# A second pair of chunks by Strassen's algorithm in four feed forward stages

## The chip, the cores and the metric

The kernel runs on one core of one Trainium2 chip, in one launch. The metric is the device time of that core in microseconds (us), lower is better. The engines are PE (TensorE, with its weight loads as PEld), DVE (VectorE), ACT (ScalarE), POOL (GpSimd) and SP (SyncE, which here only issues transfers).

## The reference, cut to what matters

Two transformer blocks in sequence on 256 tokens of width 1024, all in float32. Five of the kernel's eight stages are feed forward stages of this form (stages 0, 2, 3, 5, 7; the others are mixers):

```
D_FF = ((8 * D_MODEL // 3 + 127) // 128) * 128      # 2816
def swiglu(x, w_in, w_out):
    a, b = jnp.split(x @ w_in, 2, axis=-1)
    return (jax.nn.silu(a) * b) @ w_out
...
f = swiglu(rms_norm(h, g[0]), ffn1_w_in[l], ffn1_w_out[l])
h = h + FFN_RES * rms_norm(f, g[1])
...
ffn = jnp.dot(jax.nn.silu(jnp.dot(h2, w_ffn_gate)) * jnp.dot(h2, w_ffn_up), w_ffn_down)
```

`x` is 256 x 1024, `w_in` 1024 x 5632, `w_out` 2816 x 1024. The second block also needs `silu(c) @ w_ada` (1024 x 6144), a product with one row, which the kernel computes on the side.

## The kernel before, in words

**Splitting.** A float32 product is made of three matmuls on rounded parts: weights and activations are each written as hi + lo, and hi·hi, hi·lo and lo·hi are summed in PSUM. Every piece of weights, called a sub here (two blocks of 128 rows by 512 columns, 128x1024 on the chip), is loaded, rounded by ACT (line 549, `whi`), and its rest is taken by DVE (line 560, `wlo`). PE then runs 12 matmuls with it (lines 757, 758, 760): 2 row blocks x 2 halves of the tokens x 3. Seven split buffers (`NSPL`) let ACT and DVE run ahead of PE; `act_begin(j)` and `dve_begin(j)` split up to sub j + 4 (`ahead`), and the split of sub j waits until PE is done with sub j - 7. Raw weights come through a ring of three 1 MB buffers that SP fills (line 522): a refill waits for the `wlo` of the unit three places earlier. A unit is 1 MB, two subs.

**A feed forward stage.** The 2816 hidden columns are 11 chunks of 256; with both matrices a chunk is 512 columns, four subs, 48 matmuls, in one PSUM bank for each half of the tokens (tok 0, tok 1). Six banks (`acc`) go round in a ring, so a chunk's banks come back two chunks later. When a chunk ends, ACT takes silu of one half (line 1161), DVE multiplies by the other (`dve_gate`, line 1167) and signals `gated`, which frees the bank. Pairs of chunks are transposed on PE (line 1225) and split again by ACT and DVE (`gh`, `gl`: lines 1240, 1249) for the down product.

**Strassen.** In stages 2, 3, 5 and 7 the chunks 8 and 9 are computed together: a 256 x 1024 by 1024 x 1024 product, seen as 2 x 2 blocks, takes seven block products (p1 to p7) of 12 matmuls each instead of eight. Their subs are sums of weight blocks: POOL issues plain transfers (line 587) and accumulating ones (line 585) into the buffers `rows` (x1) and `work` (x2), and DVE makes one sum (`dve_t2`, line 576). The sums of activation blocks (`sxh`, `sxl`) are made by DVE and ACT at set places in chunks 3 to 5 (`SX_AT`, `SX_HI`, `SX_LO`; lines 618 to 640). ACT copies partial results (`act_part`, line 878), DVE subtracts them in PSUM (`dve_combine`, line 887), and both finish with `act_silu_pair` and `dve_gate_pair` (lines 1184, 1191). p1 stands before chunk 10, the other six between subs of the down product (`BESIDE`).

**On the side.** `w_ada` comes in 96 tiles (12 groups of 8), one beside a ring unit where `ADA_UNITS` allows it by the unit's number in its stage. DVE adds tile k right after a unit's last `wlo` (`ada_add`: k = 0 at line 651, the others at 654). After a group's eighth tile SP writes the sum out in four transfers (line 684), and k = 0 of the next group waits until they have landed (`s_sent`), because it overwrites the same buffer; later five small DVE instructions fold the group (`ada_sum`, lines 661 to 670).

**Order.** Every engine's program is written out in order by hand, and each engine runs its own strictly in that order; semaphores tie them together.

## Time and profile before

| | us |
|---|---|
| time, median of 3 runs | 1409.75 (1408.96 to 1410.26) |
| the profiled execution's own time | 1410.26 |
| its span in the profile | 1408.5 |
| PE busy | 1394.6 (99%) |
| DVE busy | 1003.0 (71%) |
| ACT busy | 760.9 (54%) |
| granted TensorE clock, mean | 0.999 of full |

Busy time of PE counts overlapping matmuls, so 99% says only that PE hardly ever stands idle. DVE and ACT shares are averages over stages; whether one of them is late somewhere is seen in the order of time. Idle time of an engine other than PE costs nothing unless PE waits for what is behind it.

### The profile page before, as it was taken

What the parts mean: (1) busy time and instruction counts of PE and PEld (TensorE: products, weight loads), DVE (VectorE), ACT (ScalarE), POOL (GpSimd) and SP (SyncE); (2) the same over time, 40 slices, a digit from 0 to 9 for tenths busy, and PEclk for the clock granted to TensorE, in tenths of its full rate; (3) what the DMA queues carried; (4) which work ended last, traced back from release to release, by engine and by line L of the source; (5) the groups of instructions that cost most, each with busy time, mean ns of one, the idle gap of its engine ahead of it and who ended that gap; (6) DMA issues with size and microseconds to landing.
All of it is one profiled execution on the core that took longest, in us unless ns stands there. A gap on an engine that the chain in (4) does not pass through costs nothing.

```text
span 1408.5 us, 19150 instructions
## 1 busy us (share of the span) xinstructions
PE 1394.6 (99%) x7293; PEld 1141.1 (81%) x7293; DVE 1003.0 (71%) x1350; ACT 760.9 (54%) x1080; POOL 195.4 (14%) x272
## 2 busy tenths in 40 slices
PE   9999999999999999999999999999999999999998
PEld 7888888688888888888878888888877788788886
DVE  6667666887867678676786877766568666776664
ACT  5444455665555455454755645556556634655452
POOL 1600010010001010010172101101652110000100
PEclk9999999999999999999999999999999999999999
DMA  9777756148879688787544788784745355586672
GB/s 311 245 237 234 258 183 209 61 140 267 278 193 273 212 264 258 238 231 234 182 142 150 226 272 254 196 264 143 255 149 195 120 179 179 196 252 210 170 217 92
DMA packets 228346, 294.54 MB, mean 209 GB/s; under 512 B 35156, under 2 KB 142480, under 8 KB 228256
## 3 DMA queue, kind: packets, MB, share of 16 engines
q1 hardware_dynamic: 218992, 272.04, 59.7%
q0 software_dynamic: 8832, 20.97, 6.9%
q8 instruction: 58, 0.95, 0.3%
q10 hardware_dynamic: 432, 0.32, 0.1%
q14 instruction: 32, 0.26, 0.1%
HBM read 289.09 MB, written 4.20 MB: 208 GB/s over the span
## 4 chain that ended last, share of the span: by engine, by line
PE 93%; DVE 3%; issue 2%; ACT 1%; DMA 1%; SPq 0%; POOL 0%; POOLq 0%; ACTq 0%; DVEq 0%
PE ps L757 27%; PE ps L760 27%; PE ps L758 27%; PE ps L864 2%; PE ps L863 2%; PE ps L862 2%; PE pst L1225 1%; PE pst L1041 1%; DVE wlo L560 1%; PE pst L1558 1%; DMA raw<-in_ffn_w_in_dram 0%; ACT whi L549 0%; PE ps L1505 0%; PE pst L1872 0%; DMA ada_out<-adaacc 0%
## 5 line engine op out<-in xcount | busy, mean ns | idle before, releaser
L560 DVE TENSOR_TENSOR wlo<-raw,whi 128x1024 fp32r<-128x1024 f32 (+2 forms) x450 | 540.3, 1224 | 178.4 <-ACT whi L549 174.6
L549 ACT ACTIVATE whi<-raw 128x1024 fp32r<-128x1024 f32 (+2 forms) x450 | 450.3, 1039 | 130.8 <-PE ps L760 115.6
L757 PE MATMUL ps<-whi,xh 128*128 128x512 f32 (+2 forms) x1310 | 513.7, 392 | 1.8 <-DVE wlo L560 0.9
L758 PE MATMUL ps<-wlo,xh 128*128 128x512 f32 (+2 forms) x1310 | 503.8, 385 | 0.0
L760 PE MATMUL ps<-whi,xl 128*128 128x512 f32 (+2 forms) x1310 | 495.3, 385 | 0.0
L757 PEld LDWEIGHTS ps<-whi,xh 128*128 128x128 f32 x1310 | 245.9, 188 | 56.9 <-issue 3.7
L760 PEld LDWEIGHTS ps<-whi,xl 128*128 128x128 f32 x1310 | 245.9, 188 | 49.8
L758 PEld LDWEIGHTS ps<-wlo,xh 128*128 128x128 f32 x1310 | 246.2, 188 | 46.0
L757 PE MATMUL ps<-whi,gh 128*128 128x512 f32 x440 | 172.7, 392 | 0.0
L758 PE MATMUL ps<-wlo,gh 128*128 128x512 f32 x440 | 171.3, 389 | 0.0
L760 PE MATMUL ps<-whi,gl 128*128 128x512 f32 x440 | 153.4, 389 | 0.0
L1161 ACT ACTIVATE hid<-ps,st 128x256 f32<-128x256 f32 x76 | 36.0, 473 | 164.6 <-PE ps L760 164.6
L760 PEld LDWEIGHTS ps<-whi,gl 128*128 128x128 f32 x440 | 82.6, 188 | 17.3
L757 PEld LDWEIGHTS ps<-whi,gh 128*128 128x128 f32 x440 | 82.6, 188 | 17.3 <-DVE hid L1191 0.2
L758 PEld LDWEIGHTS ps<-wlo,gh 128*128 128x128 f32 x440 | 82.7, 188 | 16.7
L981 POOL TENSOR_SCALAR st<-st 128x1 f32<-128x1 f32 x26 | 11.6, 446 | 562.4 <-ACT work L967 562.4
L1167 DVE SCALAR_TENSOR_TENSOR hid<-ps,st,hid 128x256 f32<-128x256 f32 x76 | 35.9, 482 | 70.8 <-ACT hid L1161 70.7
L654 DVE SCALAR_TENSOR_TENSOR adaacc<-adat,scol,adaacc 128x512 f32<-128x512 f32 x84 | 62.7, 747 | 6.3 <-DMA adat<-in_w_ada_dram 6.3
L1240 ACT ACTIVATE gh<-pst 128x1024 fp32r<-128x1024 f32 x25 | 25.7, 1028 | 44.6 <-PE pst L1225 44.6
L549 ACT ACTIVATE whi<-rows 128x1024 fp32r<-128x1024 f32 x32 | 32.9, 1054 | 17.9 <-PE ps L760 13.3
L560 DVE TENSOR_TENSOR wlo<-rows,whi 128x1024 fp32r<-128x1024 f32 x32 | 38.1, 1220 | 4.8 <-ACT whi L549 4.7
L1249 DVE TENSOR_TENSOR gl<-pst,gh 128x1024 fp32r<-128x1024 f32 x25 | 30.5, 1220 | 10.0 <-ACT gh L1240 10.0
(315 smaller groups left out, 1253.4 us busy)
## 6 DMA issues: line engine op xcount, KB each, us to landing
raw<-in_ffn_w_in_dram SPq DMA_DIRECT2D x150, 512.0 KB, 5.1
raw<-in_ffn_w_out_dram SPq DMA_DIRECT2D x40, 1024.0 KB, 6.4
raw<-in_w_in_dram SPq DMA_DIRECT2D x26, 1024.0 KB, 5.0
adat<-in_w_ada_dram SPq DMA_DIRECT2D x96, 256.0 KB, 5.8
raw<-in_hyb_w_in_dram SPq DMA_DIRECT2D x10, 1024.0 KB, 5.3
raw<-in_gla_w_in_dram SPq DMA_DIRECT2D x10, 1024.0 KB, 5.2
raw<-in_w_ffn_down_dram SPq DMA_DIRECT2D x10, 1024.0 KB, 7.4
rows<-in_ffn_w_in_dram POOLq DMA_DIRECT2D x18, 512.0 KB, 5.9
```

The source lines that it names most:

```text
L549: e.activation(split_of(whi, j), raw_of(j), ACT.Copy).then_inc(*whi_made.up(j))
L560: e.tensor_tensor(split_of(wlo, j), raw_of(j), split_of(whi, j).bitcast(F32), ALU.subtract).then_inc(*wlo_made.up(j))
L654: e.scalar_tensor_tensor(adaacc[:, :], adat[n % 2][:, :], sc, adaacc[:, :], ALU.mult, ALU.add).then_inc(*ada_added.up(c, k))
L757: e.matmul(ps[:, 0:n], a, whi_of(j, k), start=first and k == 0, stop=False)
L758: last = e.matmul(ps[:, 0:n], a, wlo_of(j, k), start=False, stop=False)
L760: last = e.matmul(ps[:, 0:n], b, whi_of(j, k), start=False, stop=final and k == subs[j][2] - 1)
L862: e.matmul(ps[:, :], a, whi_of(j, k), start=first and not i and not k, stop=False, skip_group_check=True)
L863: e.matmul(ps[:, :], a, wlo_of(j, k), start=False, stop=False, skip_group_check=True)
L864: last = e.matmul(ps[:, :], b, whi_of(j, k), start=False, stop=i == 1 and k == 1, skip_group_check=True)
L1161: e.activation(hb[:, tok * 512 + 256:tok * 512 + 512], acc.of(st, JC[st, c], tok)[:, 0:256], ACT.Silu, scale=rstd(("h", st, tok)) if st < ...
L1167: e.scalar_tensor_tensor(hb[:, tok * 512:tok * 512 + 256], acc.of(st, JC[st, c], tok)[:, 256:512], rstd(("h", st, tok)) if st < 7 else 1.0 ...
L1249: e.tensor_tensor(halves_of(gl[:, x]), turned_halves, halves_of(gh[:, x]).bitcast(F32), ALU.subtract).then_inc(*glo_made.up(st, c))
```

## The change

`STRASSEN` stays (2, 3, 5, 7), and in all four (`TWO`) the chunks 4 and 5 are now a second Strassen pair. Its seven products stand among the chunks of the first product; the order of a stage becomes 0, 1, p1, 2, p2, 3, p5, 6 (with p6 inside), p3, 7, p7, 10 (with p4 inside), and the pair 8, 9 has p1 moved to the start of the down product. The pair 4, 5 takes fixed PSUM banks 4, 0, 3, 2, and every single chunk from 2 on the fixed banks 1 and 5. The buffers x1 and x2 change roles for the second pair, whose p5 starts with its own plain load of a block (`pool_first`) that POOL waits for. The activation sums move forward to chunks 1 and 2. Transposes of hidden pairs move to (2, 2), (6, 3), (10, 1) and behind chunk 10. In the form of `ADA_UNITS` nothing changes, but a stage now has 29 ring units where it had 31, and so takes 21 tiles where it took 22.

```diff
         STRASSEN = (2, 3, 5, 7)
-        PAIR = 8
+        TWO = (2, 3, 5, 7)
...
+        OTHER = {"x1": "x2", "x2": "x1", "ring": "ring"}
         BESIDE = {2: ("p5",), 4: ("p6",), 6: ("p3", "p2"), 10: ("p7",), 12: ("p4",)}
+        INSIDE = {(6, 2): (4, "p6"), (10, 2): (4, "p4")}
...
         def sequence(st):
 
+            if st in TWO:
+                return (0, 1, (4, "p1"), 2, (4, "p2"), 3, (4, "p5"), 6, (4, "p3"), 7, (4, "p7"), 10)
             if st in STRASSEN:
-                return (*range(8), "p1", 10)
+                return (*range(8), (8, "p1"), 10)
             return tuple(range(11))
...
+        def pool_first(e, st, pair):
+
+            u, v = product_unit[st, pair, "p5"], product_unit[st, pair, "p1"]
+            buf, landed = buffer_of(u)
+            for half in range(2):
+                e.dma_start(buf[:, half * 1024:(half + 1) * 1024].rearrange("p (k n) -> p k n", k=2),
+                            plan[v][0][0][0][:, 2 * half:2 * half + 2, :]).then_inc(*landed[half].up(u, "first"))
+            for half in range(2):
+                e.wait_ge(*landed[half].at(u, "first"))
...
         def pool_strassen(e, st):
...
+                pool_product(e, st, 4, "p1", False)
+                split(4, "p1")
+                pool_product(e, st, 4, "p5", True)
+                e.wait_ge(*xlo_made.at(st, "sums", 1))
+                pool_product(e, st, 4, "p3", False)
+                split(4, "p6")
+                pool_product(e, st, 4, "p4", True)
+                split(4, "p3")
+                pool_product(e, st, 4, "p7", True)
+                split(4, "p7")
+                pool_first(e, st, 8)
+                pool_product(e, st, 8, "p5", True)
+                split(4, "p4")
+                pool_product(e, st, 8, "p3", False)
+            split(8, "p6")
+            pool_product(e, st, 8, "p4", True)
+            split(8, "p3")
+            pool_product(e, st, 8, "p7", True)
...
+            ta, tb_, tc, td = (4, 0, 3, 2) if pair == 4 else (0, 3, 1, 5)
...
+        def turns_at(st, c, i):
+
+            if st in TWO:
+                return {(2, 2): 0, (6, 3): 2, (10, 1): 6}.get((c, i))
+            return before(st, c) if c % 2 == 0 and i == 2 else None
...
-                mixed = c == 10 and st in STRASSEN
-                pe_chunk(e, st, JC[st, c], readers[c], at, (acc.n + 1, acc.n + 5) if mixed else (None, None))
+                mixed = st in TWO or c == 10 and st in STRASSEN
+                pe_chunk(e, st, JC[st, c], readers[c], at, (acc.n + 1, acc.n + 5) if mixed else (None, None), CSUB[st, c])
+            if st in TWO:
+                pe_hid_two(e, st, 4)
...
-        SX_AT = [(3, 0), (3, 1), (3, 2), (3, 3), (4, 0)]
-        SX_HI, SX_LO = [(5, 0), (5, 2)], [(5, 1), (5, 3)]
+        SX_AT = {False: [(3, 0), (3, 1), (3, 2), (3, 3), (4, 0)], True: [(1, 0), (1, 1), (1, 2), (1, 3), (2, 0)]}
+        SX_HI = {False: [(5, 0), (5, 2)], True: [(2, 1), (2, 2)]}
+        SX_LO = {False: [(5, 1), (5, 3)], True: [(2, 2), (2, 3)]}
+
+        COMBINE = {(2, 2): "p1", (6, 3): "p6", (10, 1): "p7"}
...
+                    if twice and (c, i) in COMBINE and c > 2:
+                        dve_combine(e, st, 4, COMBINE[c, i])
+                    if twice and (c, i) == (10, 2):
+                        dve_glo(e, st, 6)
+                        dve_gate_pair(e, st, 4, 0)
+                    if twice and (c, i) == (10, 3):
+                        dve_gate_pair(e, st, 4, 1)
```

PE in stage 3, before, from the end of chunk 2 to the first matmuls of chunk 3 (numbers are buffers; lines 757 to 760 are the three matmuls, L1225 the transposes). Left out are rows of the same kind:

```order
L757 MATMUL ps2<-whi2,xh 128x512 [waits wlo_made]
...
L760 MATMUL ps3<-whi2,xl 128x512
L757 MATMUL ps4<-whi3,xh 128x512 [waits wlo_made,gated]
...
L757 MATMUL ps5<-whi3,xh 128x512 [waits gated]
...
L757 MATMUL ps4<-whi4,xh 128x512 [waits wlo_made]
```

A chunk goes to the next pair of banks in the ring. PE in stage 3, after, at the same place, with the block product p2 of the pair 4, 5 (L925) between chunk 2 and chunk 3:

```order
L822 MATMUL ps5<-whi3,xl 128x512
L925 MATMUL ps0<-whi4,xh 128x512 [waits wlo_made,part_made]
...
L925 MATMUL ps0<-whi5,xh 128x512 [waits wlo_made]
...
L819 MATMUL ps1<-whi6,xh 128x512 [waits wlo_made,gated]
...
L819 MATMUL ps5<-whi6,xh 128x512 [waits gated]
```

Chunk 3 now writes ps1 and ps5, the banks that chunk 2 wrote, and waits there for chunk 2's gates, with 12 matmuls of p2 in between.

DVE in stage 3, before, from the gates of chunk 1 to the gates of chunk 2 (L1167 gate, L560 wlo, L654 tile of w_ada, L661 to L670 fold, L1249 gl):

```order
L654 SCALAR_TENSOR_TENSOR adaacc<-adat,scol,adaacc 128x512 [waits ada_added,s_ada1]
...
L651 TENSOR_SCALAR adaacc<-adat,scol 128x512 [waits s_sent,silu_c,s_ada0]
L560 TENSOR_TENSOR wlo<-raw,whi 128x1024 [waits whi_made] x2
L654 SCALAR_TENSOR_TENSOR adaacc<-adat,scol,adaacc 128x512 [waits ada_added,s_ada1]
L1167 SCALAR_TENSOR_TENSOR hid<-ps,st,hid 128x256 [waits silu_made] x2
L560 TENSOR_TENSOR wlo<-raw,whi 128x1024 [waits whi_made] x2
L654 SCALAR_TENSOR_TENSOR adaacc<-adat,scol,adaacc 128x512 [waits ada_added,s_ada0]
L661 TENSOR_TENSOR fold<-fold 128x256 [waits s_fold]
...
L560 TENSOR_TENSOR wlo<-raw,whi 128x1024 [waits whi_made] x2
L654 SCALAR_TENSOR_TENSOR adaacc<-adat,scol,adaacc 128x512 [waits ada_added,s_ada1]
L1249 TENSOR_TENSOR gl<-pst,gh 128x2x8x64 [waits ghi_made]
L1167 SCALAR_TENSOR_TENSOR hid<-ps,st,hid 128x256 [waits silu_made] x2
```

DVE in stage 3, after, from the last tile of a group (L716) over the gates of chunk 1 (L1233) to those of chunk 2; L591 is wlo, L713 the first tile of the next group, L689 and L692 steps of the activation sums, L702 their lo part, L1324 gl:

```order
L716 SCALAR_TENSOR_TENSOR adaacc<-adat,scol,adaacc 128x512 [waits ada_added,s_ada1]
L689 TENSOR_TENSOR work<-work 128x512 [waits summed]
L1233 SCALAR_TENSOR_TENSOR hid<-ps,st,hid 128x256 [waits silu_made] x2
L591 TENSOR_TENSOR wlo<-raw,whi 128x1024 [waits whi_made] x2
L713 TENSOR_SCALAR adaacc<-adat,scol 128x512 [waits s_sent,silu_c,s_ada0]
L591 TENSOR_TENSOR wlo<-raw,whi 128x1024 [waits whi_made]
L692 TENSOR_TENSOR work<-work 128x512 [waits summed]
...
L702 TENSOR_TENSOR sxl<-work,sxh 128x1024 [waits xhi_made]
L591 TENSOR_TENSOR wlo<-raw,whi 128x1024 [waits whi_made]
L716 SCALAR_TENSOR_TENSOR adaacc<-adat,scol,adaacc 128x512 [waits ada_added,s_ada0]
...
L702 TENSOR_TENSOR sxl<-work,sxh 128x1024 [waits xhi_made]
L1324 TENSOR_TENSOR gl<-pst,gh 128x2x8x64 [waits ghi_made]
L1233 SCALAR_TENSOR_TENSOR hid<-ps,st,hid 128x256 [waits silu_made] x2
```

The group's first tile (L651, now L713), which waits for `s_sent`, stood before the gates of chunk 1 and now stands behind them, and the steps of the activation sums have come in between the two pairs of gates.

## Rows read from the trace of the kernel before

**Rows 1.** the page, parts 1 and 4, busy times and the chain that ended last

```profile
PE 1394.6 (99%) x7293; PEld 1141.1 (81%) x7293; DVE 1003.0 (71%) x1350; ACT 760.9 (54%) x1080; POOL 195.4 (14%) x272
...
PE 93%; DVE 3%; issue 2%; ACT 1%; DMA 1%; SPq 0%; POOL 0%; POOLq 0%; ACTq 0%; DVEq 0%
```

**Rows 2.** waits, longest first: engine line waited for, us, times, longest (engines PE, DVE)

```profile
PE ps L818 <- ACT whi L549: 1.4, 1, 1.4
...
PE pst L1225 <- DVE hid L1191: 0.5, 1, 0.5
...
DVE adaacc L651 <- DMA ada_out<-adaacc: 20.9, 6, 5.0
```

**Rows 3.** windows of stages 2, 3, 5, 7: busy us (count) by engine, clock, DMA share, GB/s

```profile
305.00:481.00 176.00, 176.00 (x849) 144.56 (x848) 134.79 (x158) 94.57 (x119) 15.58 (x16) 1.00 0.82 251
487.00:665.00 178.00, 178.00 (x858) 146.34 (x857) 136.19 (x159) 96.30 (x121) 15.39 (x16) 1.00 0.80 241
782.00:958.00 176.00, 175.50 (x847) 144.13 (x846) 132.43 (x153) 94.29 (x119) 13.63 (x16) 1.00 0.82 248
1214.00:1384.00 170.00, 169.68 (x816) 138.94 (x816) 120.32 (x142) 95.49 (x125) 10.83 (x11) 1.00 0.71 217
```

**Rows 4.** timeline of ACT: silu of tok 1 in stages 3 (chunks 1, 2, 3) and 7

```profile
515.45 0.47 ACT L1161 ACTIVATE hid<-ps,st 128x256 f32<-128x256 f32 x1 [2.60 <-PE ps L760]
...
527.21 0.47 ACT L1161 ACTIVATE hid<-ps,st 128x256 f32<-128x256 f32 x1 [0.88 <-PE ps L760]
...
538.09 0.47 ACT L1161 ACTIVATE hid<-ps,st 128x256 f32<-128x256 f32 x1 [0.88 <-PE ps L760]
...
1241.55 0.38 ACT L1161 ACTIVATE hid<-ps 128x256 f32<-128x256 f32 x1 [2.36 <-PE ps L760]
```

**Rows 5.** timeline of DVE, stage 3: prices of its instructions and one wait

```profile
505.78 0.75 DVE L654 SCALAR_TENSOR_TENSOR adaacc<-adat,scol,adaacc 128x512 f32<-128x512 f32 x1
...
507.79 0.49 DVE L1167 SCALAR_TENSOR_TENSOR hid<-ps,st,hid 128x256 f32<-128x256 f32 x1 [1.27 <-ACT hid L1161]
...
514.93 0.49 DVE L651 TENSOR_SCALAR adaacc<-adat,scol 128x512 f32<-128x512 f32 x1 [3.83 <-DMA ada_out<-adaacc]
...
515.33 2.35 DVE L560 TENSOR_TENSOR wlo<-raw,whi 128x1024 fp32r<-128x1024 f32 x2
...
517.60 0.74 DVE L654 SCALAR_TENSOR_TENSOR adaacc<-adat,scol,adaacc 128x512 f32<-128x512 f32 x1
...
518.26 0.87 DVE L1167 SCALAR_TENSOR_TENSOR hid<-ps,st,hid 128x256 f32<-128x256 f32 x2
...
521.98 0.42 DVE L661 TENSOR_TENSOR fold<-fold 128x256 f32<-128x256 f32 x1
...
523.51 2.35 DVE L560 TENSOR_TENSOR wlo<-raw,whi 128x1024 fp32r<-128x1024 f32 x2
...
526.44 1.22 DVE L1249 TENSOR_TENSOR gl<-pst,gh 128x1024 fp32r<-128x1024 f32 x1
...
532.74 0.69 DVE L621 TENSOR_TENSOR work<-work 128x512 f32<-128x512 f32 x1
```

**Rows 6.** timeline of DVE, stage 7: the last gate of chunk 0

```profile
1235.17 0.43 DVE L1167 SCALAR_TENSOR_TENSOR hid<-ps,hid 128x256 f32<-128x256 f32 x1 [1.46 <-ACT hid L1161]
```

**Rows 7.** lines 585 (accumulating, whole run) and 587 (plain, 315 to 330 us): time to landing

```profile
DMA to landing us min/median/max: 5.8/9.2/12.4
...
DMA to landing us min/median/max: 4.2/4.4/4.7
```

**Rows 8.** timeline of DVE, stage 5: the same waits for a transfer out

```profile
853.63 0.75 DVE L654 SCALAR_TENSOR_TENSOR adaacc<-adat,scol,adaacc 128x512 f32<-128x512 f32 x1
...
864.95 0.49 DVE L651 TENSOR_SCALAR adaacc<-adat,scol 128x512 f32<-128x512 f32 x1 [5.02 <-DMA ada_out<-adaacc]
...
939.53 0.74 DVE L654 SCALAR_TENSOR_TENSOR adaacc<-adat,scol,adaacc 128x512 f32<-128x512 f32 x1
...
947.28 0.49 DVE L651 TENSOR_SCALAR adaacc<-adat,scol 128x512 f32<-128x512 f32 x1 [3.59 <-DMA ada_out<-adaacc]
```

275 lines of the change are left out of this document (161 added, 114 removed).

## The prediction

> **What bounds the kernel now.** I read the page first: PE is busy for 1394.6 us of the span and carries 93% of the chain that ended last, DVE 3% [rows 1]. Then the waits: PE's longest is one of 1.4 us at the start of the kernel, and inside the four stages it is 0.5 us, once [rows 2]. So time is what PE issues, plus nothing. Then the windows of the four stages that change [rows 3]: PE is busy throughout, DVE for 134.8 of 176 us in stage 2, 136.2 of 178 in stage 3, 132.4 of 176 in stage 5, 120.3 of 170 in stage 7 (77, 77, 75 and 71%), ACT for about 95. The reader is to see that DVE has a quarter left on average; whether it has that quarter where the change puts work is a question for the order of time. There the opening of a stage is the tight place: from the first tile after its wait in stage 3 to the first step of the activation sums behind chunk 3, DVE's rows follow each other without a gap (514.93 to 532.74) [rows 5], though some work of that stretch was held up by a transfer (3.83 us of waiting).
>
> **What the change takes away.** A pair of chunks costs 2 x 4 subs x 12 = 96 matmuls, seven products of 12 cost 84. That is 12 matmuls a stage, 48 in four stages. Two chunks without anything between them end 538.09 - 527.21 = 10.88 us apart [rows 4], so a matmul takes 10.88 / 48 = 0.2267 us, and 48 of them 10.9 us. The transposes are as many as before; a chunk with one group of them takes 527.21 - 515.45 = 11.76 us [rows 4], 0.88 more. The gain is therefore 10.9 us if PE stays gapless.
>
> **What it adds off PE, per stage.** Seven products need 14 splits where two chunks needed 8. On DVE a wlo takes (517.60 - 515.33) / 2 = 1.135 us from start to start, a tile of w_ada 0.66 (517.60 to 518.26), two gates about 0.8, the fold 1.53 (521.98 to 523.51), a gl or any other 128x1024 sum 1.13, a step of the activation sums 0.60 after overlap [rows 5]. Six more wlo are 6.8 us, the weight sum of 128x2048 is two such sums, 2.2, two combines 1.2, and two pair gates in place of four small ones give back 0.3: 9.9 us. DVE goes to some 144 of 173 us in stage 2. ACT gets 6 splits and three copies more, about 8 on 95 us. Both fit on average, so neither becomes the bound of a stage. POOL's transfers: 6 MB for the new pair in place of 4, and 1 MB for the second pair's own first block. Each lands 4.2 to 4.7 us after a plain issue in the opening and 5.8 to 12.4 after an accumulating one [rows 7]. Walking the order, p7 of the pair 4, 5 has the least room (its split is due about 11 us after its transfer can start, against 5.8 to 12.4), but ACT and DVE then are four subs ahead of PE, which hides even the 12.4. I take 0 for all transfers; bounds 0 and 1.4 us (12.4 less 11) a stage, if the lead has been used up.
>
> **The new wait.** Before, a chunk's banks came back two chunks later. Now chunk 3 needs the banks of chunk 2, chunk 6 those of 3, and so on, with one product between. From the last matmul of a bank's half to its next first one there are 18 others, 4.3 us from start to start. Silu and gate (0.47 and 0.49) follow the half's last matmul; with its own time I reckon 1.4 us when ACT and DVE are free. So DVE may be 2.9 us late at a gate, not more; behind the gate's wait stands all of PE. The Trainium skill speaks against such a layout (Perfetto Trace Analysis, Optimizing Tensor Performance: independent groups of matmuls should go round through different PSUM banks, so that the evacuation of one overlaps the next). By it alone each of the 16 places would show a bubble; by the rows a bubble of 0 is left wherever DVE is on time, and the sum below goes by the rows.
>
> **Where DVE is late: chunk 2 to chunk 3.** PE needs the first gate of chunk 2 at (silu of tok 1 of chunk 1, less 0.2 us) + p1 2.72 + chunk 2 with its transposes 11.76 + p2 2.72: 17.0 us after that silu. Between the last gate of chunk 0 (508.28 in stage 3, 7.17 before the silu at 515.45 [rows 4, 5]) and the gate wanted, DVE now has ten wlo 11.35, five steps of the activation sums 1.13 + 4 x 0.60, their two lo parts 2.26, gl 1.13, three gates 1.2: 19.5 us. To this come tiles and fold, which differ. It also waits 0.5 to 0.9 us for the first hi part of p1, whose transfer is just landing.
> - Stage 2: four tiles 2.6, fold 1.5: 23.6 + 0.8 - 7.17 = 17.3 us. Stop of PE 0.3 us.
> - Stage 5: four tiles, no fold: 15.6. No stop.
> - Stage 7: four tiles and a fold, and the start (1235.60) is only 5.95 us before the silu at 1241.55 [rows 4, 6], because that stage issues its opening in another order: 17.95. Stop 1.0 us.
> - Stage 3: here a group of w_ada ends in between. The next group's first tile waits until the four transfers out have landed: 514.93 - 506.53 = 8.4 us after the end of the eighth tile in stage 3 [rows 5], 864.95 - 854.38 = 10.6 and 947.28 - 940.28 = 7.0 us in stage 5 [rows 8]. Before, it stood in front of chunk 1's gates and cost nothing. Now the eighth tile ends at about 516.8, DVE comes to the first tile at 520.4 and waits until 525.2, with 12.2 us of work from there to the gate: 537.4, where PE wants it at 515.45 + 17.0 = 532.45. Stop 5.0 us; with 7.0 and 10.6 it is 3.5 and 7.2.
>
> **Other places, from the same order.** In stage 5 a group starts between the two pair gates of the pair 4, 5. With A the end of p7 on PE, the eighth tile ends at A + 7.8; 7.0 to 8.4 later plus 0.4 and 0.75 the second pair gate is done at A + 16.0 to 17.4. PE wants it for the transposes at A + 14.5 (p4, chunk 10 and one group of transposes). Stop 1.5 to 2.9, I take 2.2, and 5.1 with the 10.6. The other group start of stage 5 holds DVE up ahead of chunk 3's gates: 0 to 1.4, I take 0.3. Stage 3 has a fold ahead of its pair gate: 0 to 0.5, I take 0.2. Against this, stage 5's stop of 0.5 us before its last transposes [rows 2] goes, since no group starts there any more. Chunks 6, 7 and 10 otherwise have 1.5 us and more of room.
>
> **The sum.** Against the profiled execution, 1410.26 us (span 1408.5 and 1.8 around it): - 10.9 + 0.3 + 5.0 + 1.0 + 2.2 + 0.3 + 0.2 - 0.5 = - 2.4, so 1407.9. This execution lies 0.5 us above the median of the runs, so I forecast 1407.5 for a median. A change within 0.2% (2.8 us, 1406.9 to 1412.6) is what a measurement of this kernel can't tell from none. With the low ends (3.5 + 1.5, the rest 0, less 0.5) it is -6.4, or 1403.4; with the high ends (1.4 in stage 2 and in stage 7 for transfers besides 0.3 and 1.0, 7.2, 5.1, 1.4, 0.5) it is +6.9, or 1416.7.
>
> **Rivals.**
> 1. *The stops don't appear.* The walk packs DVE without any choice; if ACT or the transfer out is quicker by 2 us, or if the group's wait ends with the 7.0 of a calm stretch and the stage's lead takes up the rest, stops come to under 5 us: - 6 to - 10.9, 1399 to 1403.8, centre 1402. For it: PE waited for a gate only 0.5 us in the four stages of before, though DVE was loaded there too. Against it: the bank is a hard wait, and stage 3's order leaves DVE no gap.
> 2. *The stops last long enough to slow PE's clock*, which ends on the other side. Every window of the trace has a granted clock of 1.00 [rows 3], the upper level of 2.4 GHz, and PE never stood idle there for more than 0.5 us; the stop in stage 3 would be ten times that. At the lower level, 1.2 GHz, matmuls issued back to back take twice as long: a sub 5.4 instead of 2.7 us. Bounds are one sub (+ 2.7) and a chunk (+ 10.9); I take two subs and a half, + 6.8, which gives 1414.3. [...] The Trainium skill's page TensorE: Matmul & The Clock Gate (HAM oscillation) describes this mechanism, idle gaps between bursts that bring the clock down; no row of before shows it.
> 3. *The edge is DMA*, with 3 MB more in each stage: DMA share 0.82 at 251 GB/s in stage 2 [rows 3], so 7% more load gives 0.88. If landings move from 4.4 to 8 us in the opening, p1's hi part is 3.6 us late in each stage, and so is all of DVE behind it: + 3.6 in stages 2, 3 and 7, + 2.3 in stage 5, 13 in all: 1420. Against it: the same p1 transfer was issued at the same place before.
> 4. *Nothing is changed in matmuls*: excluded, the order has 48 fewer.
>
> **Chances.** Forecast (stops of 5 to 11 us) 57%, rival 1 22%, rival 2 14%, rival 3 7%. Of the forecast's 57, 22 fall below 1406.9 and 34 within 0.2%. Faster: 22 + 22 = 44%. Same: 34 and a few of rival 2, 37%. Slower: 19%. The range 1401.5 to 1414 leaves out part of rival 1 and the upper half of rivals 2 and 3. The forecast's own range is 1403.5 to 1411.
>
> **What would show it.** Waits of PE (its matmul into the chunk's banks, line 819 of the new kernel) for DVE's gate at line 1233: one of about 5 us in stage 3 between p2 and chunk 3, none there in stage 5, about 1 in stage 7; a wait of the transposes for the pair gate (line 1257) of about 2 us in stage 5; DVE's first tile (line 713) waiting 4 to 5 us for the transfer out just before the long one. I am wrong if these waits add up to under 4 or over 12 us, if PE's matmuls are not 10.9 us less, if the clock leaves 1.00, or if PE waits for wlo instead of for gates.

## The result, and the profile after

| | before | changed |
|---|---|---|
| time, median us | 1409.75 | 1442.77 (5 runs, 1439.66 to 1446.58) |
| ratio to before | | 1.0236, 95% interval 1.0225 to 1.0247 |
| profiled execution, us (its span) | 1410.26 (1408.5) | 1439.66 (1437.9) |
| matmuls of PE | 7293 | 7245 |

The change costs 33 us where a gain of 2.4 us was forecast, and the time lies outside the range. The profiled execution is the fastest of the five, 29.4 us of span above the one before; what follows explains those 29.4. The other four are slower at the same or a lower mean clock (0.985 to 0.988, the profiled one 0.988); where their further time goes is not shown. The page of the changed kernel (busy time and count, then shares of the chain that ended last; compare [rows 1]):

```profile
PE 1397.9 (97%) x7245; PEld 1140.5 (79%) x7245; DVE 1040.9 (72%) x1378; ACT 786.7 (55%) x1108; POOL 238.3 (17%) x312
...
PE 77%; DVE 9%; DMA 6%; issue 3%; SPq 2%; ACT 2%; POOL 0%; POOLq 0%; ACTq 0%; DVEq 0%
```

PE has 48 matmuls less and is busy for 3.3 us more. DVE's part of the chain has grown from 3 to 9%, that of transfers from 1 to 6%. The waits (us in total, times, longest), which stand against [rows 2]; the last line is of the kernel before:

```profile
DVE adaacc L713 <- DMA ada_out<-adaacc: 41.1, 7, 9.3
...
PE ps L819 <- DVE hid L1233: 12.9, 6, 3.4
...
DVE adaacc L716 <- DMA adat<-in_w_ada_dram: 11.3, 9, 4.7
PE pst L1300 <- DVE hid L1257: 11.2, 2, 7.7
...
PE ps L925 <- ACT ps L943: 3.1, 1, 3.1
...
DVE adaacc L654 <- DMA adat<-in_w_ada_dram: 6.3, 2, 3.2
```

PE now waits 24.1 us for DVE's gates and 3.1 us for a copy by ACT, 27.2 us where it waited 0.5. DVE's wait at a group's first tile (L713) for the transfer out has doubled, and at ordinary tiles (L716) DVE waits 11.3 us in nine places where it waited 6.3 in two (L654). PE's stops one by one, from the timeline of PE (start of the matmul, then in brackets how long PE stood before it):

```profile
349.10 0.50 PE L819 MATMUL ps<-whi,xh 128*128 128x512 f32 x1 [0.82 <-DVE hid L1233]
...
411.74 0.71 PE L1300 MATMUL pst<-cst,hid 64*128 64x64 f32 x16 [3.46 <-DVE hid L1257]
...
535.67 0.52 PE L925 MATMUL ps<-whi,xh 128*128 128x512 f32 x1 [3.07 <-ACT ps L943]
...
543.70 0.80 PE L819 MATMUL ps<-whi,xh 128*128 128x512 f32 x1 [3.43 <-DVE hid L1233]
...
593.57 0.50 PE L819 MATMUL ps<-whi,xh 128*128 128x512 f32 x1 [2.38 <-DVE hid L1233]
...
844.60 0.50 PE L819 MATMUL ps<-whi,xh 128*128 128x512 f32 x1 [1.03 <-DVE hid L1233]
...
860.87 0.50 PE L819 MATMUL ps<-whi,xh 128*128 128x512 f32 x1 [2.22 <-DVE hid L1233]
...
914.19 1.12 PE L1300 MATMUL pst<-cst,hid 64*128 64x64 f32 x16 [7.75 <-DVE hid L1257]
...
1287.74 0.80 PE L819 MATMUL ps<-whi,xh 128*128 128x512 f32 x1 [3.07 <-DVE hid L1233]
```

Two in stage 2, three in stage 3, three in stage 5, one in stage 7. At L819 PE wants a shared bank of a single chunk, at L1300 it wants the gated pair for its transposes. What DVE did ahead of the two in the middle of stage 3 (timeline of DVE; compare [rows 5]):

```profile
518.48 0.75 DVE L716 SCALAR_TENSOR_TENSOR adaacc<-adat,scol,adaacc 128x512 f32<-128x512 f32 x1
...
519.75 0.87 DVE L1233 SCALAR_TENSOR_TENSOR hid<-ps,st,hid 128x256 f32<-128x256 f32 x2
...
530.88 0.49 DVE L713 TENSOR_SCALAR adaacc<-adat,scol 128x512 f32<-128x512 f32 x1 [7.99 <-DMA ada_out<-adaacc]
...
540.90 1.22 DVE L702 TENSOR_TENSOR sxl<-work,sxh 128x1024 fp32r<-128x1024 f32 x1
542.04 1.22 DVE L1324 TENSOR_TENSOR gl<-pst,gh 128x1024 fp32r<-128x1024 f32 x1
543.17 0.87 DVE L1233 SCALAR_TENSOR_TENSOR hid<-ps,st,hid 128x256 f32<-128x256 f32 x2
```

The eighth tile ends at 519.23, DVE reaches the next group's first tile 3.66 us later and stands there for 8.0 us: the transfer out took 11.65 us where the prediction had 8.4. From 530.88 to the gate at 543.17 it is 12.3 us of work with one gap of 0.3, as forecast (12.2). ACT, which the prediction had not followed there, was held up by the same wait, because its split of the activation sums comes ahead of its copy of p1 into the bank in which p2 adds up:

```profile
533.13 1.06 ACT L697 ACTIVATE sxh<-work 128x1024 fp32r<-128x1024 f32 x1 [10.71 <-DVE work L692]
...
535.04 0.58 ACT L943 ACTIVATE ps<-ps 128x512 f32<-128x512 f32 x1
```

Then the clock. Windows of 2 us over the same place (columns as in [rows 3]):

```profile
536.00:538.00 2.00, 2.00 (x6) 1.60 (x5) 1.96 (x3) 2.00 (x3) 0.00 (x0) 0.51 0.96 301
...
544.00:546.00 2.00, 2.00 (x5) 1.52 (x5) 2.00 (x3) 0.00 (x0) 0.00 (x0) 0.50 0.93 295
...
550.00:552.00 2.00, 2.00 (x10) 1.64 (x9) 2.00 (x2) 0.35 (x1) 0.00 (x0) 1.00 0.89 324
```

After 3.1 us of standing PE works at 0.51, half of full speed, which is the level of 1.2 GHz; a window of 2 us touches 6 matmuls where it touches 10 at 1.00. With such windows over the whole span, the time lost to the lower level (1 less the granted clock, times PE's busy time, where the clock is under 0.99) is 13.1 us, in six intervals. Each begins during one of these stops or at most 1.5 us behind it. These sums are good to about 0.2 us. The Trainium skill (TensorE: Matmul & The Clock Gate, HAM oscillation) describes idle gaps between bursts that bring the clock down; here the trace agrees.

Each stage, from its first transpose of x to that of the next (stage 7: to its last matmul), adds up:

| stage | before | changed | difference | matmuls | stops | lower clock | sum |
|---|---|---|---|---|---|---|---|
| 2 | 183.6 | 187.0 | + 3.5 | - 2.7 | + 4.3 | + 1.7 | + 3.3 |
| 3 | 183.5 | 196.6 | + 13.0 | - 2.7 | + 8.9 | + 6.3 | + 12.5 |
| 5 | 182.9 | 193.1 | + 10.2 | - 2.7 | + 10.5 | + 2.1 | + 9.9 |
| 7 | 188.4 | 191.8 | + 3.5 | - 2.7 | + 3.1 | + 3.0 | + 3.3 |

(Stage 5's stops are 11.0 us less the 0.5 that it had before.) So the 10.9 us of matmuls were saved, and 27 us of stops and 13 of lower clock came on top. The experiments are about what makes DVE late.

### The profile page after: what moved, and what is told of

It is laid out like the page before. It is cut to its first block, busy times and chain, and to the rows that moved or that the text cites. A ratio compares the mean times of both kernels' runs of the same rounds, so it can differ in the third digit from the quotient of the medians.

```text
span 1437.9 us, 19194 instructions
## 1 busy us (share of the span) xinstructions
PE 1397.9 (97%) x7245; PEld 1140.5 (79%) x7245; DVE 1040.9 (72%) x1378; ACT 786.7 (55%) x1108; POOL 238.3 (17%) x312
## 4 chain that ended last, share of the span: by engine, by line
PE 77%; DVE 9%; DMA 6%; issue 3%; SPq 2%; ACT 2%; POOL 0%; POOLq 0%; ACTq 0%; DVEq 0%
PE ps L819 21%; PE ps L822 21%; PE ps L820 21%; DVE wlo L591 4%; DMA adat<-in_w_ada_dram 3%; PE ps L925 3%; PE ps L926 3%; PE ps L927 3%; DMA ada_out<-adaacc 2%; SPq L746 2%; PE pst L1107 1%; ACT whi L580 1%; PE pst L1300 1%; DVE adaacc L716 1%; PE pst L1666 1%
## 5 line engine op out<-in xcount | busy, mean ns | idle before, releaser
L591 DVE TENSOR_TENSOR wlo<-raw,whi 128x1024 fp32r<-128x1024 f32 (+3 forms) x434 | 521.4, 1225 | 167.4 <-ACT whi L580 163.6
L580 ACT ACTIVATE whi<-raw 128x1024 fp32r<-128x1024 f32 (+3 forms) x434 | 436.6, 1040 | 167.2 <-PE ps L822 132.0
L819 PE MATMUL ps<-whi,xh 128*128 128x512 f32 (+4 forms) x1182 | 467.3, 395 | 14.6 <-DVE hid L1233 12.9
L820 PE MATMUL ps<-wlo,xh 128*128 128x512 f32 (+4 forms) x1182 | 456.8, 386 | 0.0
L822 PE MATMUL ps<-whi,xl 128*128 128x512 f32 (+4 forms) x1182 | 448.2, 387 | 0.0
L819 PEld LDWEIGHTS ps<-whi,xh 128*128 128x128 f32 x1182 | 223.7, 189 | 67.4 <-DVE hid L1233 15.5
L822 PEld LDWEIGHTS ps<-whi,xl 128*128 128x128 f32 x1182 | 223.6, 189 | 45.5
L820 PEld LDWEIGHTS ps<-wlo,xh 128*128 128x128 f32 x1182 | 224.1, 190 | 41.7
L819 PE MATMUL ps<-whi,gh 128*128 128x512 f32 x440 | 172.6, 392 | 0.0
L819 PEld LDWEIGHTS ps<-whi,gh 128*128 128x128 f32 x440 | 82.6, 188 | 17.1
L716 DVE SCALAR_TENSOR_TENSOR adaacc<-adat,scol,adaacc 128x512 f32<-128x512 f32 x84 | 62.8, 747 | 11.3 <-DMA adat<-in_w_ada_dram 11.3
L591 DVE TENSOR_TENSOR wlo<-rows,whi 128x1024 fp32r<-128x1024 f32 x48 | 57.3, 1221 | 8.2 <-ACT whi L580 8.2
L1233 DVE SCALAR_TENSOR_TENSOR hid<-ps,st,hid 128x256 f32<-128x256 f32 x64 | 29.6, 480 | 41.3 <-ACT hid L1227 41.3
L580 ACT ACTIVATE whi<-work 128x1024 fp32r<-128x1024 f32 x40 | 41.5, 1060 | 32.3 <-PE ps L822 12.6
L591 DVE TENSOR_TENSOR wlo<-work,whi 128x1024 fp32r<-128x1024 f32 x40 | 47.7, 1220 | 11.3 <-ACT whi L580 11.2
```

The lines of the kernel that those rows point to most:

```text
L580: e.activation(split_of(whi, j), raw_of(j), ACT.Copy).then_inc(*whi_made.up(j))
L591: e.tensor_tensor(split_of(wlo, j), raw_of(j), split_of(whi, j).bitcast(F32), ALU.subtract).then_inc(*wlo_made.up(j))
L716: e.scalar_tensor_tensor(adaacc[:, :], adat[n % 2][:, :], sc, adaacc[:, :], ALU.mult, ALU.add).then_inc(*ada_added.up(c, k))
L819: e.matmul(ps[:, 0:n], a, whi_of(j, k), start=first and k == 0, stop=False)
L820: last = e.matmul(ps[:, 0:n], a, wlo_of(j, k), start=False, stop=False)
L822: last = e.matmul(ps[:, 0:n], b, whi_of(j, k), start=False, stop=final and k == subs[j][2] - 1)
```

## The experiments

The expectations weigh theories by letter. A: DVE's wait at a group's first tile makes the gates late. A2: any wait of DVE for a transfer of w_ada ahead of a gate does. B: DVE has too much work of its own. C and D: transfers are late as a whole, wherever the work that needs them stands. E: SP's long issue of the transfer out holds up what it issues next.

Ratios are to the kernel before, on the same chip; "stops" are PE's of 0.6 us and more in the four stages, "clock" is the time lost to the lower level, both of the profiled execution. Runs of different groups ran on different chips, so a difference between groups is surer in the ratios than in us.

| run | median us | ratio, 95% interval | stops | clock |
|---|---|---|---|---|
| changed kernel | 1442.77 | 1.0236 (1.0225 to 1.0247) | 27.2 | 13.1 |
| two_acc | 1437.49 | 1.0201 (1.0187 to 1.0215) | 21.1 | 7.1 |
| two_acc_gates_first | 1432.20 | 1.0164 (1.0150 to 1.0178) | 16.5 | 6.8 |
| two_acc_aligned | 1424.63 | 1.0105 (1.0091 to 1.0119) | 19.7 | 7.2 |
| two_acc_gates_aligned | 1422.73 | 1.0091 (1.0075 to 1.0106) | 15.7 | 7.8 |
| tiles_moved | 1432.32 | 1.0161 (1.0148 to 1.0175) | 23.8 | 4.7 |
| three_edits | 1411.03 | 1.0004 (0.9994 to 1.0014) | 8.4 | 3.3 |
| folds_moved | 1407.22 | 0.9980 (0.9970 to 0.9990) | 5.4 | 0 |
| plain_out | 1421.98 | 1.0091 (1.0077 to 1.0105) | 17.9 | 8.6 |
| plain_edits | 1408.33 | 0.9991 (0.9982 to 1.0000) | 6.1 | 1.5 |
| no_dma_wait | 1406.37 | 0.9976 (0.9966 to 0.9986) | 5.1 | 1.4 |
| no_wait_no_load | 1406.45 | 0.9975 (0.9966 to 0.9984) | 5.7 | 1.7 |
| seven_only | 1412.68 | 1.0019 (1.0010 to 1.0028) | 3.9 | 1.6 |
| five_seven | 1415.68 | 1.0048 (1.0035 to 1.0061) | 8.0 | 1.6 |
| before_two_acc | 1418.27 | 1.0063 (1.0050 to 1.0077) | 0 | 0 |
| before_moved_480 | 1418.89 | 1.0065 (1.0052 to 1.0079) | 0 | 0 |
| before_edits | 1409.08 | 0.9997 (0.9989 to 1.0006) | 0 | 0 |
| before_plain | 1412.02 | 1.0017 (1.0008 to 1.0026) | 2.6 | 0 |

**Two accumulators for w_ada**, so that a group's first tile no longer waits for the transfer out of the group just ended. They were built twice. `st_` is cut to 384 columns in both; with `mhalf` as below the tiles behind end up 1,056 bytes on, with `mhalf` as a part of `st_` (`st_[:, 376:384]`, the aligned version) 1,024 bytes:

```diff
-        adaacc = sb("adaacc", 512)
+        adaacc = [sb(f"adaacc{i}", 512) for i in range(2)]
...
-        mhalf = sb("mhalf", P)[:, 0:8]
+        mhalf = sb("mhalf", 8)
...
-                if c:
-                    e.wait_ge(*s_sent.at(c - 1))
+                if c > 1:
+                    e.wait_ge(*s_sent.at(c - 2))
```

> The changed kernel with two accumulators for w_ada, so that a group's first tile waits for the transfer out of the group before the last, which landed long ago. Theory A (the wait of DVE at a group's first tile is what makes the gates late): the stops of PE in stage 3 (3.1, 3.4 and 2.4 us), stage 5 (2.2 and 7.7) and stage 7 (3.1) shrink to 1.5 us or less each, those of stage 2 (0.8 and 3.5, the latter behind a tile that lands late) stay; stops of 27 us become 5 to 8, the intervals at the lower clock level go with them except the one in stage 2, and the time is 1403 to 1410. Theory B (DVE has too much work of its own for two banks that come back after one product): the stops stay within a third, only with another releaser, and the time is over 1430. Theory C (the DMA queues are the bound, the group's wait is only where it shows): DVE waits instead for tiles of w_ada and ACT for raw weights, time 1420 to 1435.

> The kernel before with the same two accumulators, a control. Its DVE waits 20.9 us at six group starts, but PE only once, 0.5 us, for a gate behind one. Theories A, B and C all expect no change within 0.1% (1409 to 1411), DVE's wait at the first tile gone. If it is faster by more than 1 us, a part of what the first run gains is not owed to the changed order.

> Two accumulators again, but all tiles behind them stay at multiples of 512 bytes as in the changed kernel (in the first version the tiles from fold on stood 480 bytes off, and the 1,500 or so matmuls that read gh, gl, sxh and sxl took 5 to 6 ns longer each, 9 us in all, in the control too). If the address is the cause of that, this is 8 to 9 us faster than the first version, 1428 to 1430, with the same stops (about 21 us). If the extra time came from something else in the edit, 1436 to 1438.

> The kernel before with one small unused stretch of on-chip memory taken out, so that the tiles from fold on (gh, gl, sxh, sxl among them) start 480 bytes earlier; nothing else is changed. If the address costs 5 to 6 ns for each matmul that loads its stationary operand from such a tile, as in the control with two accumulators: 1417.5 to 1419. If that control's 8.9 us came from the second accumulator: 1409 to 1410.

(The kernels show the shifts of 1,056, 1,024 and 480 bytes; that the old places are all multiples of 512 bytes, as the expectations say, they don't show.) The first control was 8.9 us slower, which no theory had, without any new wait. It comes from the address alone: before_moved_480 moves the tiles by 480 bytes and changes nothing else, and costs 9.3 us. before_moved_480 (groups of PE's matmuls by shape: busy us, mean ns):

```profile
L757 PE MATMUL ps<-whi,xh 128*128 128x512 f32 x1246 | 494.4, 397 | 0.7 <-ACT xh L1080 0.3 <-DVE wlo L560 0.3
...
L757 PE MATMUL ps<-whi,gh 128*128 128x512 f32 x440 | 175.3, 399 | 0.0
...
L862 PE MATMUL ps<-whi,sxh 128*128 128x512 f32 x64 | 25.3, 396 | 0.0
```

and the kernel before:

```profile
L757 PE MATMUL ps<-whi,gh 128*128 128x512 f32 x440 | 172.7, 392 | 0.0
...
L862 PE MATMUL ps<-whi,sxh 128*128 128x512 f32 x64 | 24.9, 389 | 0.0
```

Matmuls whose stationary operand lies in a moved tile (gh, gl, sxh, sxl) take 6 to 7 ns more, those with xh, which did not move, the same; 1,500 of them are 9 us. In the changed kernel 1,704 matmuls read such tiles, and PE's busy time differs by 11.1 us between two_acc and two_acc_aligned (1402.2 and 1391.1); so the aligned version came out 12.9 us faster, where 8 to 9 were expected. The kernels with two_acc's form carry this and are not compared with the others. Without it two accumulators take 18.1 us off the changed kernel. Theory A had asked for 1403 to 1410 and is wrong as it stood: 7.5 us of stops went, but others grew. Theory C had 1420 to 1435 and DVE waiting for tiles in place of the transfer out, and both came true. The waits that took the place of the old one (DVE and PE of two_acc_aligned):

```profile
409.83 0.75 DVE L716 SCALAR_TENSOR_TENSOR adaacc<-adat,scol,adaacc 128x512 f32<-128x512 f32 x1 [4.70 <-DMA adat<-in_w_ada_dram]
...
528.00 0.75 DVE L716 SCALAR_TENSOR_TENSOR adaacc<-adat,scol,adaacc 128x512 f32<-128x512 f32 x1 [2.28 <-DMA adat<-in_w_ada_dram]
...
599.67 0.42 DVE L723 TENSOR_TENSOR fold<-fold 128x256 f32<-128x256 f32 x1 [5.27 <-DMA fold<-ada_out]
```

```profile
411.39 0.85 PE L1300 MATMUL pst<-cst,hid 64*128 64x64 f32 x16 [3.45 <-DVE hid L1257]
...
539.63 0.80 PE L819 MATMUL ps<-whi,xh 128*128 128x512 f32 x1 [4.71 <-DVE hid L1233]
...
607.15 1.12 PE L1300 MATMUL pst<-cst,hid 64*128 64x64 f32 x16 [5.86 <-DVE hid L1257]
```

DVE now waits near the same places for the next thing that a transfer has to bring: a tile, or a fold. Whether all transfers are late, raw weights too, or only what DVE needs of w_ada matters, is for no_dma_wait to tell.

**Silu and gates ahead of gh and gl** in chunks 2, 6 and 10 (on DVE; the same on ACT):

```diff
-                if c % 2 == 0:
+                if c % 2 == 0 and not twice:
                     dve_glo(e, st, before(st, c))
                 dve_gate(e, st, c, 0)
                 dve_gate(e, st, c, 1)
+                if c % 2 == 0 and twice:
+                    dve_glo(e, st, before(st, c))
```

> Two accumulators, and in the four stages silu and gates of chunks 2, 6 and 10 ahead of the splits of the transposed pair (gh on ACT, gl on DVE) instead of behind them. Theory A: what is left at the start of chunk 3 is DVE's own work ahead of the gate, and gl is 1.13 us of it, so the stops there (0.8, about 1, 1.0, about 1) go; 1 to 4 us faster than with two accumulators alone. Theory B: the same sign but larger, 5 us and more. Theory C: no change.

> Two accumulators (at multiples of 512 bytes) and silu and gates ahead of gh and gl, tiles of w_ada where the changed kernel has them. In the version 480 bytes off the gates' place was worth 5.3 us and took the stops of 0.97, 1.76 and 1.67 us at the start of chunk 3 in stages 2, 5 and 7 away. The same is expected here: 1418 to 1421, and what it is above the run with three edits is the price of the tiles' places, 17 to 21 us by theory A2, under 8 by theory D.

The stops of about 1 us at the start of chunk 3 shrink or go, as theory A had it, for 5.3 us in one pair of kernels and 1.9 in the other (whose two intervals overlap); the expected 1418 to 1421 was missed by 2 us.

**No wait for w_ada at all.** DVE's tile and fold instructions read and write tiles of their own. What is still waited for is the tile two places earlier, by DVE and by SP, and the fold before. w_ada's product is left out by this, so the kernel's output is not the reference's:

```diff
+        idle = sb("idle", 512)
...
-            e.wait_ge(*s_ada[n % 2].at(n))
+            if n > 1:
+                e.wait_ge(*s_ada[n % 2].at(n - 2))
...
-                e.scalar_tensor_tensor(adaacc[:, :], adat[n % 2][:, :], sc, adaacc[:, :], ...
+                e.scalar_tensor_tensor(idle[:, :], adaacc[:, :], sc, idle[:, :], ...
```

> The changed kernel, where DVE's work on w_ada has the same instructions, sizes and places, and all transfers run as before, but DVE reads and writes tiles of its own and so never waits for a tile of w_ada, a transfer out or the fold (the sums of w_ada are left out, they are zero). Theory A2 (all the large stops come from DVE waiting for w_ada's transfers, in two accumulators the tiles in place of the transfer out): only stops of 0.3 to 1.5 us stay at the start of chunk 3, 2 to 5 us in all, no interval at the lower clock level, 1401 to 1404. Theory B (DVE's own work is too much): 12 us and more of stops stay, over 1412. Theory C (DMA as a whole is late, raw weights and sums too): stops of PE behind wlo, over 1410.

This run tells the theories apart: it is 36.4 us faster than the changed kernel, and DVE waits for no transfer of w_ada. PE's stops that are left:

```profile
348.89 0.50 PE L834 MATMUL ps<-whi,xh 128*128 128x512 f32 x1 [0.67 <-DVE hid L1248]
...
532.83 0.79 PE L834 MATMUL ps<-whi,xh 128*128 128x512 f32 x1 [2.76 <-DVE hid L1248]
...
1257.22 0.50 PE L834 MATMUL ps<-whi,xh 128*128 128x512 f32 x1 [1.65 <-DVE hid L1248]
```

All are at the start of chunk 3. Theory A2 is right in the main and not in all. The time is below the 1412 and 1410 over which B and C had it, but 2.4 us above A2's upper end; two stops are longer than its 1.5 us, and one is followed by the lower clock (1.4 us lost). In stage 3 the stop is for the most part not DVE's own work: ACT waits 2.3 us for raw weights, DVE 2.7 behind it, and PE stops for 2.8.

```profile
523.07 1.06 ACT L581 ACTIVATE whi<-raw 128x1024 fp32r<-128x1024 f32 x1 [2.28 <-DMA raw<-in_ffn_w_in_dram]
...
524.16 1.23 DVE L592 TENSOR_TENSOR wlo<-raw,whi 128x1024 fp32r<-128x1024 f32 x1 [2.67 <-ACT whi L581]
```

**Without most of w_ada's loads** (16 of 512 columns of a tile loaded, the rest as in the last; the product is left out here too):

> The changed kernel with DVE's work on w_ada in tiles of its own and without waits for transfers, as before, and now w_ada's tiles are not loaded either except for 16 of 512 columns (w_ada's sums are left out, 5.3 MB less a stage). Left with the transfers on were stops of 0.7, 2.8 and 1.7 us at the start of chunk 3 and waits of DVE of 0.9 to 2.3 us for POOL's second block. Theory A2 (what is left is DVE's own work ahead of the gates): stops and time stay within 1 us, 1405 to 1407. Theory D: DVE's waits for POOL's blocks go to under 0.5 us, the stops shrink by half, 1402 to 1404.

Same time, nearly the same stops; DVE's waits for POOL's second block are gone (all but one of 0.8 us), and PE's stops didn't shrink. Theory A2 for the stops, D only for DVE's waits. It wasn't the bytes of the tiles that held the rest up: ACT still waits 2.35 us for raw weights in stage 3. The transfers out and the folds stayed in this run as they were, so nothing is said of them.

**Where the tiles and folds stand**, by the table alone:

```diff
-        beside_ffn = *range(3, 19), *range(24, 30)
+        beside_ffn = (3, 4, 5, *range(9, 17), *range(19, 30))
...
-                                   if ring_place[q][1] >= 5 and ring_place[q][1] + 1 in ...
+                                   if ring_place[q][1] >= 9 and ring_place[q][1] + 1 in ...
```

> The changed kernel with one accumulator as it is, but the 21 tiles of w_ada of each of the stages 2, 3 and 5 (9 in stage 7) moved by the table alone: none beside the units 6, 7, 8 (ahead of the gates of chunk 2) and 17, 18 (ahead of the pair gates of 4, 5), beside the units 19 to 23 of the down product instead, and no fold before unit 9. Theory A2 (DVE waits for w_ada's transfers in front of gates): stops of PE at the start of chunk 3 and at the pair gates go except where a group's first tile still waits; 27 us become 5 to 12, lower clock 2 to 5 us instead of 13, time 1404 to 1418. Theory D (DMA bursts make whatever DVE needs late, wherever the tiles stand): over 1425, stops behind other tiles.

> The changed kernel with all three: two accumulators (tiles behind them at multiples of 512 bytes), silu and gates ahead of gh and gl in chunks 2, 6, 10, and the tiles of w_ada moved by the table. Theory A2: stops of under 3 us in all, no lower clock, so nearly the whole of the 10.9 us: 1398.5 to 1402. Theory D: 1410 and more. Below 1406 it beats the kernel before by more than can be owed to noise.

> The kernel before with two accumulators (at multiples of 512 bytes) and the same table of tiles (22 a stage there), a control for the run with three edits: what of its gain is not owed to the second Strassen pair. PE waits there 0.5 us for a gate, so all theories: 1408.5 to 1410. If it is faster by 2 us or more, the comparison of the three edits must be made against this one.

With one accumulator the table brings 10.5 us, not 25 to 39: the waits at group starts moved along, and one of DVE became 12.3 us long, with PE's stop of 8.2 behind it. The time is above 1425, where theory D had it. With all three edits the kernel is level with the one before, 31.7 us faster than the changed one; theory A2's 1398.5 to 1402 was missed, D's "1410 and more" met. Against two_acc_gates_aligned, on the same chip, the tiles' places bring 11.7 us, between A2's 17 to 21 and D's under 8. The control shows that these edits alone do nothing to the kernel before (1409.08), so they are worth something only to a kernel whose gates are urgent. The largest stop left stood behind a fold (DVE, three_edits):

```profile
400.45 0.74 DVE L716 SCALAR_TENSOR_TENSOR adaacc<-adat,scol,adaacc 128x512 f32<-128x512 f32 x1
405.88 0.42 DVE L723 TENSOR_TENSOR fold<-fold 128x256 f32<-128x256 f32 x1 [4.68 <-DMA fold<-ada_out]
...
409.68 0.74 DVE L1257 SCALAR_TENSOR_TENSOR hid<-ps,st,hid 128x512 f32<-128x512 f32 x1
```

The fold's place was then restricted, `ring_place[q][1] in (*range(9, 15), *range(19, 30))`:

> The version with three edits, and no fold of w_ada beside the units 15 to 18 either (the one in stage 2 waited 4.7 us for its transfer, right ahead of the pair gates, and PE stopped for 4.3 us behind it, with 1.6 us of lower clock after it). Theory A2: that stop goes to under 1 us, 5 to 6 us faster than with three edits: 1404 to 1407. Theory D (bursts of DMA make whatever DVE needs late, wherever it stands): the stop moves to the next thing that DVE waits for, 1409 to 1412.

PE's three longest stops in this kernel:

```profile
362.40 0.50 PE L819 MATMUL ps<-whi,xh 128*128 128x512 f32 x1 [1.04 <-DVE hid L1233]
...
546.22 0.50 PE L819 MATMUL ps<-whi,xh 128*128 128x512 f32 x1 [1.40 <-DVE hid L1233]
...
1269.10 0.50 PE L819 MATMUL ps<-whi,xh 128*128 128x512 f32 x1 [1.30 <-DVE hid L1233]
```

No interval at the lower clock in the profiled execution, and 1407.22 us: 0.2 us above the range of theory A2, 1.8 below that of D, 0.2% faster than the kernel before, 2.5% faster than the changed one. The stop did shrink to 1 us, but the gain is 3.8 us, not 5 to 6. The profiled execution (1404.64) is one of the fastest of eight that reach up to 1409.54; what the slower ones lose is not shown. It is the only form with the reference's full computation here whose interval lies below 1. Its DVE still waits 3.3 to 4.1 us for a tile in three places (437.79, 626.80, 915.09), with no stop of PE over 1.0 us behind them. So both theories hold a part: the transfers are late wherever the work stands (D), and they cost something only ahead of a gate that PE is about to need (A2).

**Fewer stages**, `TWO = (7,)` in the changed kernel, and `TWO = (5, 7)` in the last one:

> The change in stage 7 alone (stages 2, 3 and 5 as before, so 22 tiles of w_ada each again, and stage 7 has 6 left where it had 9). 12 matmuls less are 2.7 us. Theory A2: with no group start ahead of chunk 3 in stage 7 one stop of about 1 us is left there: 1407.5 to 1408.5. Theory B: stops of 3 us as in the full change with the clock drop behind them, 1411 to 1413. Theory C: 1409 to 1411.

> The same, with the second pair by Strassen in stages 5 and 7 alone, where the version with three edits had no stop over 0.6 us. 24 matmuls less are 5.4 us. Theory A2: gapless, 1409.1 (the control with the same edits) less 5.4: 1403.5 to 1404.5. Theory D: 1406 and more.

A2 missed both. seven_only lies in theory B's range: in stage 7 a stop of 2.15 us came, with no group start ahead of it and only one wait of 0.55 us for a tile, so nearly all DVE's own work, and 1.6 us at the lower clock behind it. A second stop, 1.70 us, came in stage 5, which has the old order: the wait for the transfer out before its last transposes was 4.8 us where it was 3.6 before. The two stops and the clock are more than the 2.7 saved. five_seven lies in D's range, 11 us above A2's. In its stages of the old order stand two stops of 1.2 and 1.6 us behind late tiles, and in stage 5 another tile landed late right ahead of a pair gate:

```profile
926.60 0.75 DVE L716 SCALAR_TENSOR_TENSOR adaacc<-adat,scol,adaacc 128x512 f32<-128x512 f32 x1 [6.08 <-DMA adat<-in_w_ada_dram]
```

PE behind it:

```profile
931.89 0.79 PE L819 MATMUL ps<-whi,gh 128*128 128x512 f32 x1 [4.17 <-DVE hid L1257]
```

**The transfer out as one piece of 2 KB runs**: DVE writes the eighth tile's sum into a second buffer in the order that memory wants.

```diff
+            elif k == 7:
...
+                for q in range(4):
+                    last = e.scalar_tensor_tensor(adaq[:, q * P:(q + 1) * P].rearrange("p (b n) -> p b n", b=4),
+                                                  of_q(adat[n % 2], q), sc, of_q(adaacc, q), ALU.mult, ALU.add)
...
-                for b in range(4):
-                    e.dma_start(ada_out[c].rearrange("p (q b n) -> b p q n", q=4, b=4)[b], ...
+                e.dma_start(ada_out[c], adaq[:, :]).then_inc(*s_sent.up(c))
```

> The changed kernel, where DVE writes the eighth tile's sum into a second buffer in the order that the memory wants (four instructions of 128x128 in place of one of 128x512), so that the transfer out is one of 2 KB runs in place of four of 128-byte runs, and no group's first tile waits. Tiles, folds and gates stand where the changed kernel has them. Two accumulators alone gave 1424.6 us. Theory E (SP's issue of the small pieces holds up everything that it issues next): SP's issue falls from 7 to 9 us to under 1, the waits of DVE for tiles and folds go to under 1.5 us, stops of PE 19.7 us become 4 to 7, time 1404 to 1409. Theory D (the DMA engines are full there, whatever the pieces): 1420 to 1425.

> The same transfer out, with the three edits and the moved folds of the best version so far (1407.2): silu and gates first, tiles and folds by the table. Theory E: nearly gapless, 1399 to 1402. Theory D: 1405 to 1408.

> The kernel before with the same transfer out, tiles and folds, the control for both. PE waits there 0.5 us for a gate, so by either theory 1408.5 to 1410. What plain_edits is below this one is what the second Strassen pair itself is worth, 10.9 us by its matmuls.

Theory E falls; the two times are those of D, or 0.3 us above it. SP's part did go, first the changed kernel, then plain_out (issue start, us that SP was busy):

```profile
520.38 7.41 SPq L746 DMA_DIRECT2D ada_out<-adaacc  x4
```

```profile
519.33 0.76 SPq L757 DMA_DIRECT2D ada_out<-adaq  x1
```

but the tiles were about as late as in two_acc_aligned (2.85 us at 528.38, 4.10 at 409.30), the one transfer took up to 14.8 us to land, and the time is 2.6 us below two accumulators alone, with intervals that overlap. The control is 2.6 us above the kernel before, where 1408.5 to 1410 was expected, and two stops of PE, 1.3 and 1.4 us behind late tiles, make that up; five_seven has such stops at the same two places with the moved folds and without this transfer out, so the folds' places are the likelier cause. Against its control plain_edits is 3.7 us faster, and that is what the second pair is worth here of its 10.9.

What makes transfers slow in those stretches stays open. The DMA engines' share from 520 to 528 us (1.10 in the changed kernel, 1.05 in plain_out) is not much above that of before at its own group starts (1.01 and 1.05), and the bytes of w_ada's tiles aren't it either. The 12.6 MB more that the changed kernel moves in all (307.1 and 294.5) were not tested apart.

**What a stop does to the clock**, three stops of set length in stage 0 of the kernel before:

```diff
+                if j in STOPS:
+                    e.wait_ge(*stopped.at(j, STOPS[j] - 1))
```

> The kernel before with three stops of PE of set length in stage 0 (ahead of chunks 5, 7 and 9), where it has none: PE waits there for a chain of 1, 3 and 5 small POOL instructions that starts when the chunk ahead has ended. Measures what a stop does to the clock. By the changed kernel's rows (stops of 0.8 to 2.2 us left the clock at 1.00, those of 2.4 us and more were followed by 4 to 12 us at 0.5): if the chains take about 0.9, 2.5 and 4.0 us, the first costs its own length and the other two their own length and 2 to 6 us more. If the drop has nothing to do with the stop, the clock stays at 1.00 and the time grows by the sum of the stops, about 7.5 us.

One execution, 1419.89 us:

```profile
67.68 0.47 PE L760 MATMUL ps<-whi,xh 128*128 128x512 f32 x1 [0.60 <-POOL mhalf L3051]
...
92.17 0.47 PE L760 MATMUL ps<-whi,xh 128*128 128x512 f32 x1 [1.58 <-POOL mhalf L3051]
...
119.34 0.76 PE L760 MATMUL ps<-whi,xh 128*128 128x512 f32 x1 [4.26 <-POOL mhalf L3051]
```

```profile
118.00:120.00 2.00, 0.66 (x2) 0.59 (x3) 2.00 (x3) 0.42 (x1) 1.11 (x2) 0.59 0.00 0
120.00:122.00 2.00, 2.00 (x6) 1.55 (x5) 0.76 (x1) 0.00 (x0) 0.00 (x0) 0.50 0.96 240
...
124.00:126.00 2.00, 2.00 (x7) 1.58 (x7) 0.02 (x1) 1.06 (x1) 0.00 (x0) 0.70 0.04 13
```

The first two cost their own length (the clock stays at 1.00 in every window up to 118 us). During the third the clock fell, and 2.9 us were lost at 0.5. The sum, 6.4 us of stops and 2.9, is 9.3 of the 9.4 us by which the span is longer. So a stop can do it, and it need not be DVE's. The second came out at 1.6 us, not the 2.5 that was meant, so this run says nothing of lengths between 1.6 and 4.3 us.

## Why the prediction was wrong, point by point

The step that failed is the pair of terms for what PE loses. The sum had 9.0 us of stops (+ 0.3 + 5.0 + 1.0 + 2.2 + 0.3 + 0.2) and nothing for the clock; the profiled execution has 27.2 us of stops and 13.1 at the lower level. The mechanism, late gates behind DVE's waits for w_ada's transfers, was right, and its size was not.

| place where PE stops | forecast | measured | what DVE (or ACT) stood at just before |
|---|---|---|---|
| stage 2, start of chunk 3 | 0.3 | 0.82 | a tile, 0.8 |
| stage 2, pair gates | 0 | 3.46 | a tile, 4.7 |
| stage 3, ACT's copy for p2 | 0 | 3.07 | group start, 8.0 |
| stage 3, start of chunk 3 | 5.0 | 3.43 | the same |
| stage 3, start of chunk 10 | 0 | 2.38 | group start, 7.1 |
| stage 3, pair gate | 0.2 | 0 | |
| stage 5, start of chunk 3 | 0 | 1.03 | tiles, 1.7 and 0.6 |
| stage 5, start of chunk 6 | 0.3 | 2.22 | group start, 5.2 |
| stage 5, pair gate | 2.2 | 7.75 | group start, 9.3 |
| stage 7, start of chunk 3 | 1.0 | 3.07 | group start, 3.9 |

- **The gain of 10.9 us** was right: 48 matmuls fewer, and with that term the table by stage closes within 0.5 us.
- **The wait at the group start** was the right mechanism in the right place (between the gates of chunks 1 and 2 of stage 3), and mis-sized: 11.65 us from the eighth tile to the landing, not 8.4, beyond even the high bound of 10.6. Ahead of the pair gate of stage 5 the same took 13.3 us, and DVE waited 9.25. The durations had been read from a kernel in which the four stages moved less by POOL; that this is why they grew was not shown.
- **Places missed.** Stage 3's second group start, ahead of chunk 7's gates; ACT's copy behind its split of the sums; stage 7's group start between the gates of chunk 0; and in stage 2 an ordinary tile ahead of the pair gates. "Tiles" stood in the sum with 0.66 us each and no wait, although a tile's wait of 3 us stood in the trace of before, harmless there.
- **DVE's own work** was short of the truth too. In stage 7 the forecast has 1.0 us; its own terms (23.6 + 0.8 - 5.95) give 18.45 and a stop of 1.5, not 17.95. Without any wait for w_ada 1.65 us are left there (no_dma_wait), and with no group start ahead 2.15 (seven_only).
- **Room of 2.9 us at a bank** was right: of the 16 places where a chunk takes over its predecessor's banks, six show a stop, 12.9 us in all, and ten none. The Trainium skill's advice to go round through different banks (Perfetto Trace Analysis, Optimizing Tensor Performance) does not tell the six from the ten. The other 14.3 us are no stops at such a bank: PE waits there for the gated pair or for ACT's copy.
- **The clock** was put at nothing in the main sum. Rival 2 had the mechanism, with 14% and a price of 6.8 us. It was treated as another case beside the forecast, when it is what follows from the forecast's own stops: six intervals, 13.1 us. The upper bound of 1416.7 held all late ends together and no clock at all.
- **Rival 3** (transfers) was priced at p1's block, for which ACT waited at most 1.1 us. What came late were the small transfers of w_ada, on which nothing of the products hangs but DVE's order. In that the rival was nearer than the 7% it got.

Measured against what could have been had: without any wait for w_ada 1406.4, with the best order 1407.2. So about 36 of the 44 us between the changed kernel and a gapless one (1409.75 - 10.9 = 1398.9) are owed to DVE standing at transfers of w_ada ahead of gates, together with the clock behind it. Of the last 7.5, 6.5 show in the profiled execution of no_dma_wait as stops of 0.7 to 2.8 us at the start of chunk 3 and the clock behind one; part of that is DVE's own work, and in stage 3 nearly all is raw weights.

## What to carry to other kernels

Before buffers are made scarcer for the busy engine, list every wait of the engine that frees them, harmless ones too, and ask for each what stands behind it: a wait costs nothing only while its place does. Side work that depends on transfers belongs behind urgent releases in a strict order, not ahead of them; the places of tiles and folds in a table were worth 15.5 us here (1422.73 to 1407.22), the algorithm 10.9. And a forecast with stops of this size (the shortest with a lower clock behind it was 1.7 us, in two_acc) should carry the clock's price in its main sum, not in a rival.

## What the runs showed of the hardware that was not expected

- Moving the tiles of a stationary operand by 480 bytes made each 128x512 matmul that loads from them 6 to 7 ns longer (389 to 396, 392 to 399 ns), 0.65% of the whole time.
- Stops of equal length did not do the same to the clock. In the changed kernel 2.22 us (at 860.87) left it at 1.00 and 2.38 us (at 593.57) did not; in tiles_moved 3.42 us (before 397.81) left it at 1.00, in two_acc_gates_aligned 1.76 us (before 902.43) did not. What the runs have in common is that each interval at the lower level before PE's last matmul begins during a stop or within 1.5 us behind it; what else decides it is open.
- Four transfers of 64 KB kept SP busy for 2.6 to 12.4 us in the changed kernel and 2.6 to 4.8 in the kernel before (7.4 and 4.4 in stage 3). Written as one transfer with long runs they took 0.8 in the same place, without landing sooner (6.6 us at the median, up to 14.8).
